# A diffusion trunk on one core: filter transforms folded on mirrored positions, magnitudes on ScalarE, taps of layer 1 between transforms

## What the reference computes

```python
h = jnp.sin(fr * (feats @ w1 + b1))
h = jnp.sin(fr * (h @ w2 + b2))
h = (h @ w3).reshape(L, HY_ORDER, 2, HY_WIDTH)          # order, forward/backward
h = h * decay[:, None, None, :]
h_fwd, h_bwd = h[:, :, 0], h[:, :, 1]
h_full = concatenate([h_fwd, zeros(1), h_bwd[1:][::-1]])
h_full = h_full / sum(abs(h_full), axis=0)
return rfft(h_full, n=2 * L)
```

## Time and profile before

| | |
|---|---|
| median of 3 runs | 3044.76 us |
| the profiled execution | 3044.86 us |
| its span | 3043.1 us |
| granted TensorE clock, mean | 0.971 |
| TensorE busy | 2871.4 us, 94% |
| DVE busy | 1458.8 us, 48% |
| GpSimd busy | 1542.4 us, 51% |
| ScalarE busy | 715.3 us, 24% |

### The profile page before, as it was taken

How to read it: one execution, slowest core, us unless ns; L and a number is a source line. 1 busy time by engine, 2 the same in 40 slices (tenths; PEclk the granted TensorE clock), 3 DMA queues, 4 the chain that set the end, 5 groups by cost and what they waited for, 6 DMA issues and landing times.

```text
span 3043.1 us, 42914 instructions
## 1 busy us (share of the span) xinstructions
PE 2871.4 (94%) x17792; PEld 2577.3 (85%) x17792; DVE 1458.8 (48%) x2373; ACT 715.3 (24%) x1356; POOL 1542.4 (51%) x577
## 2 busy tenths in 40 slices
PE   5998988999999998999999989999999999999998
PEld 1445868798888898999999959797888898999998
DVE  6885477442454434458654572442454434421113
ACT  1113112313655212000111111323565212100010
POOL 1001604065443575778876706255433575777775
PEclk9899999899999999999999999999999999999999
DMA  5432216021111222345432322021111232322222
GB/s 183 149 110 97 91 63 212 18 75 62 51 51 51 81 88 102 113 128 171 148 116 63 100 90 87 25 73 63 51 51 44 82 94 98 104 71 76 77 75 79
DMA packets 80087, 270.93 MB, mean 89 GB/s; under 512 B 9332, under 2 KB 14964, under 8 KB 78101
## 3 DMA queue, kind: packets, MB, share of 16 engines
q1 hardware_dynamic: 50140, 176.96, 18.2%
q10 hardware_dynamic: 29752, 91.23, 8.8%
HBM read 244.56 MB, written 23.59 MB: 88 GB/s over the span
## 4 chain that ended last, share of the span: by engine, by line
PE 82%; DVE 9%; ACT 3%; issue 2%; DVEq 1%; DMA 1%; POOL 1%; POOLq 0%; ACTq 0%
PE PS L475 49%; PE PS L805 9%; PE PS L538 4%; PE PS L607 2%; PE PS L852 2%; PE PS L485 2%; PE PS L749 2%; PE PS L824 1%; PE PS L733 1%; PE PS L577 1%; DVE adap L1377 1%; PE PS L720 1%; PE PS L829 1%; DMA ada<-in_w_ada 1%; PE PS L672 1%
## 5 line engine op out<-in xcount | busy, mean ns | idle before, releaser
L457 POOL TENSOR_SCALAR whi<-wraw 128x1024 fp32r<-128x1024 f32 x281 | 803.2, 2858 | 1298.2 <-PE PS L475 577.3
L459 POOL TENSOR_TENSOR wlo<-wraw,whi 128x1024 fp32r<-128x1024 f32 x292 | 739.0, 2531 | 178.6 <-ACT whi L1149 137.2
L475 PE MATMUL PS<-hhi,whi 128*128 128x320 f32 x2432 | 559.5, 311 | 19.6 <-POOL wlo L459 19.4
L475 PE MATMUL PS<-hlo,whi 128*128 128x320 f32 x2432 | 556.8, 310 | 0.0
L475 PE MATMUL PS<-hhi,wlo 128*128 128x320 f32 x2432 | 556.5, 310 | 0.0
L475 PEld LDWEIGHTS PS<-hhi,whi 128*128 128x128 f32 x2432 | 409.0, 189 | 22.4 <-POOL wlo L459 11.1
L475 PEld LDWEIGHTS PS<-hlo,whi 128*128 128x128 f32 x2432 | 409.7, 189 | 0.0
L475 PEld LDWEIGHTS PS<-hhi,wlo 128*128 128x128 f32 x2432 | 409.0, 189 | 0.0
L1377 DVE CUSTOM_DVE_ANT_0 adap<-ada,cond 128x1024 f32<-128x1024 f32 x192 | 336.4, 1752 | 38.8 <-DMA ada<-in_w_ada 16.1
L1792 DVE TENSOR_TENSOR gact<-silu,PS 128x640 f32<-128x640 f32 x44 | 36.1, 821 | 333.7 <-ACT silu L1296 333.7
L1296 ACT ACTIVATE silu<-PS 128x640 f32<-128x640 f32 x44 | 31.0, 705 | 662.2 <-PE PS L475 658.9
(11 more groups left out here) (268 smaller groups left out, 5025.8 us busy)
## 6 DMA issues: line engine op xcount, KB each, us to landing
wraw<-in_w_strips SPq DMA_DIRECT2D x292, 512.0 KB, 3.5
ada<-in_w_ada ACTq DMA_DIRECT2D x72, 512.0 KB, 4.6
ada<-in_w_ada SPq DMA_DIRECT2D x24, 512.0 KB, 3.6
spectra<-hst ACTq DMA_DIRECT2D x48, 256.0 KB, 2.0
hld<-spectra ACTq DMA_DIRECT2D x8, 768.0 KB, 5.1
hld<-spectra ACTq DMA_DIRECT2D x12, 512.0 KB, 3.6
part<-hacc ACTq DMA_DIRECT2D x8, 640.0 KB, 3.4
macc<-part ACTq DMA_DIRECT2D x8, 640.0 KB, 3.9
```

Of the source, the lines that this page charges most:

```text
L457: nc.gpsimd.tensor_scalar(hi, raw, 1.0, None, ALU.mult)
L459: nc.gpsimd.tensor_tensor(lo, raw, hi, ALU.subtract).then_inc(w_split, 1)
L475: ins = pe.matmul(out[:, h, :], w[:, kt, :], mv[:, h * HALF:(h + 1) * HALF], start=start and m == 0, stop=stop and m == 2)
```

## The change

* The two small weights, the biases and frequencies, and two sign columns come in one tensor `fpar`; `fw3` is repeated on both partition halves. SP loads them second and third. The loads of the modulation rows wait for the last sine and the last weights, since their slots now overlie those tiles.
* Layer 0's network runs through before layer 1's. ScalarE adds the bias (`mlp_keep`), DVE only reduces the argument, `mlp_sin` takes the sine. The second layer is computed on both partition halves.
* Sum and difference of forward and backward taps come from combined weights (`filter_weights`): the product gives them directly, so that `even_odd` isn't there any more. The zeroing of a row goes too.
* The latent positions are stored mirrored (n and 512 - n in tiles that stand two apart). `filter_fold` adds and subtracts these, so that a latent output is a product over two tiles, for three outputs of the first half with a one-row product besides.
* Magnitudes of sum and difference are taken by ScalarE (`taps_abs`), four instructions a unit; the larger of the two by DVE (`filter_larger`, 128x2560); `filter_norm` sums five tiles for each unit.
* The taps of layer 1 are made one order at a time between transforms. The modulation rows go in groups of 3, 6, 3 and 12, the last twelve behind the norm's reciprocal. The norm's squares have their own tiles.

```diff
+            sp.dma_start(fpar[:, :], a["fpar"]).then_inc(s_fpar, 16)
+            sp.dma_start(fw3[:, :, :, :], a["fw3"][0]).then_inc(s_fw3[0], 16)
...
-            for m in range(ADA_SLOTS[0]):
-                ada_load(m)
             sp.dma_start(x[:, :, :], a["x_in"]).then_inc(s_xin, 16)
             for n in range(3):
                 strip_load(n)
+            sp.wait_ge(s_wts, DEPTH)
+            sp.wait_ge(s_fsin, 2 * DEPTH)
+            for m in range(ADA_SLOTS[0]):
+                ada_load(m)
...
-            def filter_norm(lay):
-                pe.wait_ge(s_l1in, lay + 1)
+            def filter_norm(lay, o):
+                pe.wait_ge(s_l1in, 2 * lay + o + 1)
+                for seg, tiles in enumerate(((0,), (1, 2, 3, 4))):
+                    for c in range(KB):
+                        col = 16 * lay + 8 * o + 4 * seg + c
+                        for i in tiles:
+                            ins = pe.matmul(PS[:, 7, col:col + 1], tabs[:, 0, i, c * 128:(c + 1) * 128],
+                                            ones[:, 0:1], start=(i == tiles[0]), stop=(i == tiles[-1]))
...
-                    tiles = [0] if fc == 0 else [1, 2, 3, 4]
...
+                        which = 2 * half + (fc > 2)
+                        terms = [((ctab if kind == "A" else stab)[:, r, cols], fold4[:, which, r, :]) for r in range(2)]
+                        if kind == "A" and fc == 2:
+                            terms.append((one, fold4[0:1, 1, 0, :]))
+                        elif kind == "A" and fc > 2:
+                            terms.append((one, taps[0:1, o, 0, 0, :]))
...
+            mlp(0, 0, 3)
+            mlp(0, 1, 3)
+            mlp(1, 0, 1)
+            filter_taps(0, 0)
+            filter_taps(0, 1)
...
             filter_spectra(0, 0, 0)
+            pe.wait_ge(s_hev, 20)
+            mlp(1, 1, 3)
             filter_spectra(0, 0, 1)
             filter_spectra(0, 1, 0)
-            filter_taps(1)
+            filter_taps(1, 0)
+            filter_norm(0, 0)
             filter_spectra(0, 1, 1)
             filter_spectra(1, 0, 0)
-            filter_norm(1)
+            filter_taps(1, 1)
+            filter_norm(0, 1)
             filter_spectra(1, 0, 1)
+            filter_norm(1, 0)
             filter_spectra(1, 1, 0)
             for h in range(2):
                 norm_sums(0, h)
+            filter_norm(1, 1)
+            for h in range(2):
                 norm_spread(0, h)
             filter_spectra(1, 1, 1)
...
+            def taps_abs(lay, o):
+                u = 2 * lay + o
+                act.wait_ge(s_hev, 10 * u + 10)
+                if u:
+                    act.wait_ge(s_l1, u)
+                for d in range(2):
+                    A(tabs[:, d, 0, :], ctaps[:, o, d, :], ACT.Abs)
+                    ins = A(tabs[:, d, 1:NT, :], taps[:, o, d, :, :], ACT.Abs)
+                ins.then_inc(s_abs, 1)
...
+            for u in range(2 * DEPTH):
+                for n in range(12):
+                    keep_spectrum(u // 2, u % 2, n)
+                    if u == 0 and n == 4:
+                        mlp_sin(1, 0)
+                    elif u == 0 and n == N_A - 1:
+                        mlp_keep(1, 1, 3)
+                    elif u == 0 and n == 11:
+                        mlp_sin(1, 1)
+                        taps_abs(0, 0)
+                    elif u == 1 and n == N_A - 1:
+                        taps_abs(0, 1)
+                    elif u == 2 and n == N_A - 1:
+                        taps_abs(1, 0)
+                    elif u == 3 and n == 2:
+                        taps_abs(1, 1)
...
+            def filter_fold(lay, o, half):
+                near, far = taps[:, o, half, 0:2, :], taps[:, o, half, 2:4, :]
+                for i, op in ((0, ALU.subtract if half else ALU.add), (1, ALU.add if half else ALU.subtract)):
+                    ins = V.tensor_tensor(fold4[:, 2 * half + i], near, far, op)
+                ins.then_inc(s_fold, 1)
+            def filter_larger(lay, o):
+                dve.wait_ge(s_abs, 2 * lay + o + 1)
+                V.tensor_tensor(tabs[:, 0], tabs[:, 0], tabs[:, 1], ALU.max).then_inc(s_l1in, 1)
...
             filter_keep(0, 0)
-            even_odd(0, 0, 0)
+            filter_fold(0, 0, 0)
             filter_keep(0, 1)
+            filter_fold(0, 0, 1)
+            filter_arg(1, 0)
+            filter_fold(0, 1, 0)
+            filter_arg(1, 1)
+            filter_weights(1)
+            filter_larger(0, 0)
+            filter_fold(0, 1, 1)
+            dots(0, 3)
             filter_keep(1, 0)
+            filter_larger(0, 1)
+            filter_fold(1, 0, 0)
+            dots(3, 9)
             filter_keep(1, 1)
+            filter_fold(1, 0, 1)
+            filter_larger(1, 0)
+            filter_fold(1, 1, 0)
+            dots(9, 12)
+            filter_larger(1, 1)
+            filter_fold(1, 1, 1)
+            for k in range(1, KD + 1):
+                add_squares(0, k)
             dve.wait_ge(s_const, 16 * 8)
+            for h in range(2):
+                norm_recip(0, h)
+            dots(12, N_ADA1)
             modulation(0, 0, N_ADA1)
             norm_scale(0, 0)
```

More of the change, by code:

```diff
@@ L546, in norm_sums @@
                 for b, c0 in enumerate(BLOCKS):
-                    ins = pe.matmul(pair(2)[:, h, b:b + 1], ssum[:, h * HALF + c0:h * HALF + c0 + 128], ones[:, 0:1],
+                    ins = pe.matmul(pair(2)[:, h, b:b + 1], (ssum_later if nrm else ssum_first)[:, h * HALF + c0:h * HALF + c0 + 128], ones[:, 0:1],
                                     start=True, stop=True)
@@ L564, in mlp, with filter_taps @@
                 ins.then_inc(s_fmm, 1)
[L566 to L574, removed]
+            def filter_taps(lay, o):
+                pe.wait_ge(s_fsin, 2 * lay + 2)
+                pe.wait_ge(s_fev, 2 * lay + 2)
+                pe.wait_ge(s_wts, lay + 1)
+                for n in range(10):
+                    i, d = TAP_ORDER[n // 2], n % 2
+                    g = 20 * lay + 10 * o + n
@@ L592, in filter_spectra @@
                 u = 2 * lay + o
-                pe.wait_ge(s_heo, 2 * u + half + 1)
+                pe.wait_ge(s_fold, 2 * u + half + 1)
+                one = ones[0:1, 0:128]
                 for n in (range(N_A, 12) if half else range(N_A)):
@@ L608, in filter_spectra @@
+                    for r, (w, h) in enumerate(terms):
+                        ins = pe.matmul(out, w, h, start=(r == 0), stop=(r == len(terms) - 1))
                     ins.then_inc(s_sp, 1)
             pe.wait_ge(s_feats, 16)
-            pe.wait_ge(s_fpar, 16 * 3 * DEPTH)
-            mlp(0, 0)
-            mlp(1, 0)
-            mlp(0, 1)
-            mlp(1, 1)
-            filter_taps(0)
+            pe.wait_ge(s_fpar, 16)
+            mlp(0, 0, 3)
+            mlp(0, 1, 3)
+            mlp(1, 0, 1)
@@ L1407, in filter_arg, with filter_weights @@
                     dve.drain()
                 V.tensor_scalar(arg, arg, PI_BELOW, -PI_BELOW, ALU.min, ALU.max).then_inc(s_farg, 1)
+            def filter_weights(lay):
+                dve.wait_ge(s_fw3[lay], 16)
+                V.tensor_scalar(fw3[:, 1], fw3[:, 1], fpar[:, FP_SIGN:FP_SIGN + 1], None, ALU.mult)
+                dve.drain()
+                V.scalar_tensor_tensor(wsum[:, :, :], fw3[:, 0], fpar[:, FP_TOP:FP_TOP + 1], fw3[:, 1], ALU.mult, ALU.add)
+                dve.drain()
+                V.scalar_tensor_tensor(fw3[:, 0], fw3[:, 0], fpar[:, FP_SIGN:FP_SIGN + 1], fw3[:, 1],
+                                       ALU.mult, ALU.subtract).then_inc(s_wts, 1)
@@ L1446, in filter_linv @@
-            def filter_linv(lay):
-                dve.wait_ge(s_l1, lay + 1)
-                V.reciprocal(linvs[:, lay], PS[:, 7, 0:16])
-            for lay in range(DEPTH):
-                V.memset(farg[lay][HID:128, :], 0.0)
-            V.memset(fw3[HID:128, :, :], 0.0)
-            dve.wait_ge(s_fpar, 16 * 3 * DEPTH)
-            for n in range(2):
-                for lay in range(DEPTH):
-                    filter_arg(lay, n)
+                near, far = taps[:, o, half, 0:2, :], taps[:, o, half, 2:4, :]
@@ L1457, in _, with dots @@
+            def dots(m0, m1):
+                for m in range(m0, m1):
+                    ada_dot(0, m, m)
+            for lay in range(DEPTH):
+                V.memset(hid[lay][HID:128, :], 0.0)
+            filter_arg(0, 0)
+            dve.wait_ge(s_fpar, 16)
+            filter_weights(0)
+            filter_arg(0, 1)
             dve.wait_ge(s_csig, 1)
@@ L1493, in _ @@
                 if lay == 0:
-                    for h in range(2):
-                        norm_recip(0, h)
                     for h in range(2):
```

255 lines of the change are left out of this document (122 added, 133 removed).

## The result

| | before | after |
|---|---|---|
| median us (lowest to highest) | 3044.76 (3043.33 to 3044.78) | 3026.24 (3024.40 to 3027.13) |
| profiled execution, its span | 3044.86, 3043.1 | 3024.40, 3022.6 |
| GpSimd released for strip 2 | 288.91 | 262.97 |
| mean granted clock | 0.971 | 0.967 |

The ratio is 0.994 (95% interval 0.9922 to 0.9957): 18.5 us faster where 24.4 were forecast (3026.2 against 3020.5, inside the forecast's own range). The release came 25.9 us earlier, so the new order of time came out within 1.5 us; 5.5 us of it were given back later in the profiled execution (spans 3043.1 - 3022.6 = 20.5). The median of the changed kernel is 1.8 us above its profiled execution (3026.24 against 3024.40), which leads from 20.5 to 18.5.

What follows compares the result with a forecast made beforehand. Ahead of GpSimd's release for strip 2, TensorE and DVE bound the kernel in turn; TensorE bounds the rest. Release 28.7 us earlier less 4.3 for the clock is 24.4: 3044.9 - 24.4 = 3020.5 us, own range 3009 to 3032, 8-in-10 range 3003 to 3038.

Steps and rivals of the forecast that it cites:

- Start: Small network and first taps: weights land at 5.0 us, first tap kept at 28.4 instead of 47.15, 18.8 us earlier.
- Transforms and magnitudes: Filter units: 39 products become 24, 52 us less TensorE; ScalarE's magnitudes add 5.0 us after output 11 in unit 0.
- about 11 us: Sign: DVE idle this long behind the taps of (1,0), with ScalarE's magnitudes as releaser.
- One-row products: Three a unit in the transforms, counted as dear as full ones; bounds for all 12 are 0 and 10.4 us.
- Rows: Twelve modulation rows on DVE behind the norm's reciprocal, from about 204 us: 5.4 + 10 x 3.2 = 37.4 us.
- TensorE's pause: Sign: TensorE stands about 30 us ahead of the first strip.
- Norm: End of the stage: `norm_apply` holds DVE 17.0 us to 260.2, so strip 1's second half starts 28.7 us earlier.
- 4.3 for the clock: Deduction in us for TensorE at a lower clock behind pauses and sums, and for starting the strips after a pause.
- anything behind strip 2: Sign of being wrong: the prediction fails if anything after strip 2 moves.
- The clock rival: About 55 us of TensorE on the chain run at 1.2 GHz throughout: +51 us, about 3070; chance 4%.
- The little gain: Dearer hand-overs, late first DMA or slower rows take 12 to 20 us: 3033 to 3041, middle 3037; chance 18%.
- DVE's work alone: DVE's work sets the stage's end if waits for ScalarE and filter sums go: 2966, half gone 3000; chance 10%.

Runs made afterwards that it cites:

- doubled magnitudes: Changed kernel with ScalarE computing each unit's four magnitudes twice: 3044.34 us, ratio 0.9996 against the kernel before.
- unfolded products: Changed kernel with each latent transform's two products issued twice and the one-row products dropped (outputs not the reference's): 3050.11 us, ratio 1.0007 against the kernel before.
- first pair of traces: Profiled executions of the kernel before and the changed kernel, both unmodified, from the main measurement: 3044.86 and 3024.40 us.
- in the second: Kernel before and changed kernel, both unmodified, profiled again on one other chip: 3044.92 us (one execution) and 3026.75 us, ratio 0.994.
- The two runs with the old pace of the projections: Changed kernel with working tiles 512 bytes off: 3026.74 us, ratio 0.9939; the same 480 added bytes with modulation rows spread into DVE's waits: 2990.14 us, ratio 0.983.

## Why the prediction was right, and where it was not

- **Start.** Forecast: weights at 5.0, first tap kept at 28.4. Measured: 3.65 and 27.30. The landing was 1.4 us earlier. Behind it two misses cancel, which is luck: the taps of (0,0) took 7.8 us (27.30 to 35.05) where 9.8 stood in the sum, and the first fold cost 2.1 us more than its price, while GpSimd was splitting a strip. The Trainium skill, page SBUF — State Buffer, section "SBUF: two separate sides", says that a DVE operation with two SBUF inputs and a GpSimd operation that reads SBUF lock each other out of their shared ports. The rows at 35.14 and 35.41 agree: of the fold's two instructions the first took 1.2 us as everywhere, GpSimd's 3.15 where it takes 2.4 alone, and the second fold instruction 3.36, ending 1.1 us behind GpSimd's end. One after another, as an estimate from these rows, they are 1.2 + 2.4 + 1.2 = 4.8 us where the prediction had 2.4. The taps of (0,1) then began behind a pause of TensorE, at a granted clock of 0.50 for 6 us, and took 10.8 us, not 9.4.
- **Transforms and magnitudes.** Forecast and measured starts of `filter_larger`: 78.4 and 80.03, 114.1 and 112.22, 159.4 and 156.35, 179.9 and 177.79. The three later ones are early because the taps of (1,0) took 7.7 us (forecast 9.5), and because the first three blocks of sums took 4.5 to 5.8 us, where the rows' 0.165 an instruction, read at a granted clock of 0.65, had given 6.6 for 40. The idle of DVE "about 11 us" behind taps (1,0) was 9.81, with the magnitudes as releaser and the sums behind them. One-row products are as dear as full ones, as counted (the two instructions of one take 1.12 us from start to end, those of a full one 1.02 to 1.12). The doubled magnitudes and the unfolded products confirm both terms on the path: 20.4 us of 20.6, and 23.3 of 52.
- **Rows.** Twelve from 205.07 to 243.00, 37.9 us, forecast 37.4, and 3.2 us each behind the first two. TensorE's pause was 29.95 us (forecast 30).
- **Norm.** First to last `norm_apply` 243.82 to 261.89, 18.1 us against 17.0: in the old row its first four instructions had run ahead of the wait, so that the price left them out. GpSimd was released at 262.97, and 288.91 - 262.97 = 25.9 earlier, against 28.7 less 4.3 for the clock = 24.4. The loss to the clock was small, as weighted: the last sums ran at 1.2 GHz (8.67 us, 2.1 more than the 6.6 in the sum), and the taps of (1,1) at a mean between the two levels. With the clock's 4.3 the forecast release was 264.5, and it came 1.5 us ahead of that.
- **What failed: "anything behind strip 2".** The prediction took the rest of the kernel as unchanged, without a term for it, and named its moving as a sign of being wrong; by that sign it was wrong there. The lead fell from 25.9 to 20.5 us in the first pair of traces and from 29.1 to 19.0 in the second. 3.2 us of it are the value projections, by a new tile's place (shown by the shift in the kernel before). The clock is not the rest: its loss behind the release is the same before and after within 2 us. TensorE's pauses there grew by 4 to 5 us (2759.6 - 2637.4 against 2754.1 - 2635.8 us in the first pair), and most of that stands at one place, the long convolution's transform back (`isin`). In the waits of the whole execution (total us, times, longest us), first before and then after:

```profile
PE PS L688 <- DVE yr L1532: 2.4, 4, 0.6
```

```profile
PE PS L713 <- DVE yr L1599: 5.9, 4, 1.7
DVE yt L1596 <- DMA hld<-spectra: 3.9, 4, 1.2
```

TensorE waits there for DVE's product with the spectra, and DVE now waits for the load of the fifth and last spectrum tile of each order. It lands 3.4 to 4.0 us behind its issue in both runs of the kernel before and 4.3 to 5.0 in both of the changed one. That is 3.5 us of TensorE's 4 in the first pair and 4.1 of 5 in the second (6.5 against 2.4). All eleven traces of the changed kernel and its variants have this DVE wait, 2.7 to 4.5 us in all, and the kernel before has none; shifted by 32 bytes it has 0.2, so it isn't the tile's place. Why the load lands later stays open. The two runs with the old pace of the projections gave 10.3 and 5.0 us back all the same.
- **Rivals.** The clock rival did not come, but the argument against it was misread: transforms of the old kernel did not always run at 1.00. The window 213 to 216 in the earlier trace rows is the transforms right behind the sums, at 0.52, and those from 115 to 120 us ran at 0.50 as well; new transforms behind sums did so again (206.4 to 210.3 at 0.50). The little gain (3033 to 3041) and "DVE's work alone" (3000) did not come; but the latter's place was right. It named the waits that the program order makes, and when rows fill them the time goes to 2991, below even its half-way price of 3000.

## What to carry to other kernels

In a stage where three engines hand work to each other, ask what each one still has queued behind its last wait: here twelve independent rows at the tail cost 34 us, and moving them into the waits was worth 1.6 to 1.9 times the change itself. Removing one wait by reordering mostly moved it here. And compare the lead at several points behind the edited stage: here an added tile moved the working tiles and changed the pace of instructions that the diff does not touch, and a load that the diff does not touch landed later.

## What the runs showed of the hardware

- A 512-column matmul of the value projections followed its neighbour in 0.2267 us or in 0.2333 us and the SBUF place of the tiles alone moved it from the one to the other: 32 and 64 bytes off the old place were slow, 512 bytes off was fast.
- A block of 40 one-column products took 4.52 us at a granted clock of 1.00 and 8.67 us at 0.50, in windows of TensorE alone of the kernel after:

```profile
161.30:165.70 4.40, 4.40 (x42) 1.00 0.46 136
...
194.20:202.70 8.50, 8.50 (x41) 0.50 0.00 0
```

- A run's time goes with its mean granted clock: of the six runs of the kernel at 512 bytes off five had 0.962 to 0.966 and took 3024 to 3031 us, one had 0.971 and took 3012. With that spread a term of 3 us can be read from the trace but not from the time.
